# A two-block transformer step on one core: another order of DVE's work beside the keys and values, and side work ahead of the low half in 64 slots of a layer instead of 16

## The reference, cut to what matters

```python
for i in range(DEPTH):                                   # DEPTH = 2, "the layers"
    u = rms_norm(h, norm_g[i]); z = u @ w_in[i]
    o_a = mla_mixer(...)                                 # latent attention
    o_b = dsa_mixer(...)                                 # index scores, top 64 keys, attention
    o_c = diff_mixer(...)                                # difference of two attentions
    mixed = concat([o_a*silu(g_a), o_b*silu(g_b), o_c*silu(g_c)])
    h = h + mixed @ w_o[i]
    h = h + (p[i] @ w_ple[i]) * sigmoid(h @ w_pg[i])
h = rms_norm(h, final_g)
# second block
sh1, sc1, gt1, sh2, sc2, gt2 = split(silu(c) @ w_ada + b_ada)      # the "ada" rows, and
csh1, csc1, ...              = split(silu(c_ctx) @ w_ada + b_ada)  # the same for the context
rq, rk, rv, rg, mq, mk, mv, mo, mg, gr, gm = split_in(modulate(x, norm1_g, sh1, sc1) @ w_in)
crq, crk, ...                              = split_in(modulate(ctx, ...) @ w_in)
# retention scan and mLSTM scan, both directions; merge; then a PEER layer (top-16 experts)
```

## Time and profile before

| | us |
|---|---|
| three timed executions | 3944.96, 3946.69, 3958.2 |
| their median | 3946.69 |
| the profiled execution | 3957.74 |
| its span, first to last instruction | 3955.9 |
| PE busy in it | 3773.8 (95%) |
| DVE busy in it | 2352.2 (59%) |
| ACT busy in it | 1549.7 (39%) |

### The profile page before, as it was taken

The page is one execution under the profiler, slowest core; times in us unless marked ns, Lnnn a source line. Parts: engine busy times, 40 slices in busy tenths (PEclk is TensorE's granted clock), DMA queues, the critical chain, the costliest instruction groups (busy, mean ns, idle before and its releaser), DMA issues.

```text
span 3955.9 us, 49916 instructions
## 1 busy us (share of the span) xinstructions
PE 3773.8 (95%) x21042; PEld 3213.1 (81%) x21042; DVE 2352.2 (59%) x3127; ACT 1549.7 (39%) x1518; POOL 101.0 (3%) x145
## 2 busy tenths in 40 slices
PE   8999999999999679799999989999999999999998
PEld 6776777777777467697888889999999999988886
DVE  3455654436554366647664558867655565567777
ACT  3443544333443331125543343345533333333333
POOL 0000000000000000001000000000000000000000
PEclk8999999999999889899999999999999999999999
DMA  5545565645555436634356644555666666666664
GB/s 207 194 167 193 195 235 188 248 151 192 200 213 210 169 146 251 240 128 149 133 182 238 222 141 175 192 203 218 237 231 219 222 221 220 233 227 243 232 241 173
DMA packets 117959, 799.30 MB, mean 202 GB/s; under 512 B 13137, under 2 KB 13521, under 8 KB 29457
## 3 DMA queue, kind: packets, MB, share of 16 engines
q1 hardware_dynamic: 96704, 692.73, 48.3%
q0 software_dynamic: 18768, 82.96, 5.6%
q10 hardware_dynamic: 2304, 20.97, 1.3%
HBM read 752.57 MB, written 44.04 MB: 201 GB/s over the span
## 4 chain that ended last, share of the span: by engine, by line
PE 52%; DVE 6%; DMA 3%; ACT 2%; issue 2%; DVEq 0%; ACTq 0%; POOLq 0%; POOL 0%; SPq 0%
PE ps L289 16%; PE ps L291 16%; PE ps L290 16%; DMA ring<-in_stream_dram 3%; DVE ring_r L303 2%; PE ps L1676 1%; DVE z L2786 1%; ACT high L297 1%; PE ps L1535 1%; DVE z L3133 0%; DVE act L2897 0%; PE ps L1412 0%; PE ps L1484 0%; PE ps L1498 0%; DVE z L3129 0%
## 5 line engine op out<-in xcount | busy, mean ns | idle before, releaser
L297 ACT CAST high<-ring 128x2048 fp32r<-128x2048 f32 x384 | 733.7, 1912 | 1333.4 <-DMA ring<-in_stream_dram 1328.3
L303 DVE TENSOR_TENSOR ring_r<-ring,high 128x2048 fp32r<-128x2048 f32 x384 | 878.9, 2291 | 632.6 <-ACT high L297 629.0
L291 PE MATMUL ps<-high,act_r 128*128 128x512 f32 x1888 | 742.7, 393 | 0.0
L289 PE MATMUL ps<-high,z_r 128*128 128x512 f32 x1856 | 733.2, 395 | 1.4 <-DVE z L3251 1.2
L290 PE MATMUL ps<-ring_r,z_r 128*128 128x512 f32 x1856 | 727.3, 392 | 0.0
L290 PE MATMUL ps<-act_r,high 128*128 128x256 f32 x2496 | 707.8, 284 | 0.0
L2309 DVE TENSOR_TENSOR ring_r<-ring,high 128x2048 fp32r<-128x2048 f32 x176 | 402.6, 2290 | 458.4 <-ACT high L1784 456.8
L289 PE MATMUL ps<-act_r,high 128*128 128x256 f32 x2304 | 657.0, 285 | 9.8 <-DVE ring_r L303 9.4
L291 PE MATMUL ps<-act_r,ring_r 128*128 128x256 f32 x2304 | 652.9, 283 | 0.0
L289 PE MATMUL ps<-high,h_r 128*128 128x512 f32 x1472 | 598.7, 407 | 47.3 <-DVE ring_r L2309 17.6
L290 PE MATMUL ps<-ring_r,h_r 128*128 128x512 f32 x1472 | 579.4, 394 | 0.0
(11 more groups left out here) (474 smaller groups left out, 3172.3 us busy)
## 6 DMA issues: line engine op xcount, KB each, us to landing
ring<-in_stream_dram SPq DMA_DIRECT2D x656, 1024.0 KB, 4.8
hidden<-z POOLq DMA_DIRECT2D x32, 512.0 KB, 3.8
gate_matrix<-z ACTq DMA_DIRECT2D x8, 2048.0 KB, 6.4
r<-gate_matrix POOLq DMA_DIRECT2D x32, 512.0 KB, 6.7
z<-hidden POOLq DMA_DIRECT2D x32, 512.0 KB, 7.1
r<-in_w_ple_dram POOLq DMA_DIRECT2D x2, 2048.0 KB, 9.7
merge_gates<-r ACTq DMA_DIRECT2D x8, 512.0 KB, 5.1
r<-merge_gates POOLq DMA_DIRECT2D x4, 1024.0 KB, 5.2
```

What stands on the lines that cost most here:

```text
L289: pe.matmul(out, lhs[0], rhs[0], start=start, stop=False)
L291: return pe.matmul(out, lhs[1], rhs[0], start=False, stop=stop)
L297: sc.copy(high[:, j, :], ring[:, j, :]).then_inc(piece_high[j], 1)
L303: dve.tensor_tensor(ring_r[:, j, :], ring[:, j, :], high[:, j, :], ALU.subtract).then_inc(piece_low[j], 1)
```

## The change

There are four edits. First, in kv and mvmk DVE's work is written as one rule for every piece: after the low half of piece i+3 come a1(i+1) and a0(i+2), and then the low half of piece i+4. DVE's evacuation of a chunk stands behind the low half of the next chunk's first piece (before: of its second), and ACT's behind the cast of the next chunk's second piece (before: of its third). SP's loop is rewritten in the same form, and its list of transfers stays what it was. Second, `SIDE_FIRST` becomes 14 to 77. Third, the scan's first product no longer waits for `evac[1]`. Fourth, that wait stands before the transposes beside the scan's second piece.

```diff
-        SIDE_FIRST = range(38, 54)
+        SIDE_FIRST = range(14, 78)
...
+                        if q == 1:
+                            pe.wait_ge(evac[1], EVAC0["rgmo"])
                             turn_pairs(head_src, 8, 4, rt_full)
...
                         if c == 0:
                             pe.wait_ge(evac[0], e0)
-                            pe.wait_ge(evac[1], e0)
... ACT
-                    for m in range(4):
-                        split_act(sc, kv_chunk(m), (3,))
-                        split_act(sc, kv_chunk(m + 1), range(3))
-                        sc.wait_ge(piece_used[3], place(kv_chunk(m), 1, 1))
-                        out_kv(m // 2, m % 2)
+                    for i in range(PIECES - 1, kv_out_at(3)):
+                        split_act(sc, kv_chunk(i // PIECES), (i % PIECES,))
+                        m = (i + 1 - kv_out_at(0)) // PIECES
+                        if m >= 0 and i + 1 == kv_out_at(m):
+                            sc.wait_ge(piece_used[3], place(kv_chunk(m), 1, 1))
+                            out_kv(m // 2, m % 2)
... DVE
                     def stream_kv(m, evacuate):
-                        ada_part(m, 0, 0)
-                        low(m, 3)
-                        ada_part(m, 1, 0)
-                        ada_part(m, 0, 1)
-                        low(m + 1, 0)
-                        ada_part(m, 1, 1)
-                        ada_part(m, 0, 2)
-                        low(m + 1, 1)
-                        dve.wait_ge(piece_used[3], place(kv_chunk(m), 1, 1))
-                        evacuate()
-                        ada_part(m, 1, 2)
-                        ada_part(m, 0, 3)
-                        low(m + 1, 2)
-                        ada_part(m, 1, 3)
+                        for i in range(PIECES * m, PIECES * (m + 1)):
+                            ada_at(1, i + 1)
+                            ada_at(0, i + 2)
+                            low_at(i + PIECES)
+                            if i % PIECES == 0:
+                                dve.wait_ge(piece_used[3], place(kv_chunk(m), 1, 1))
+                                evacuate()
...
+                    ada_at(0, 0)
+                    low_at(PIECES - 1)
+                    ada_at(1, 0)
+                    ada_at(0, 1)
...
                     stream_kv(4, keep_early)
-                    split_dve(dve, kv_chunk(5), (3,))
                     split_dve(dve, kv_chunk(6), range(3))
```

More of the change, by code:

```diff
@@ L276, in ada_used, with kv_out_at @@
             return sum(kv_chunk(m)) + 2 + i
+        def kv_out_at(m):
+            return PIECES * (m + 1) + 2
         def ada_sums(n):
@@ L941, in load_ada, with load_at @@
                 sp.dma_start(ring[:, j, :], t["stream"][ada_place(ADA_L + 2 * m + i), j]).then_inc(piece_full[j], 16)
[L943 to L958, removed]
+            def load_at(i):
+                load_weights(i // PIECES, i % PIECES)
+            for i in range(PIECES - 1):
+                load_at(i)
+            load_ada(0, 0, 0)
+            load_at(PIECES - 1)
+            load_ada(0, 1, 0)
+            load_ada(0, 0, 1)
+            for i in range(KV_ADA * PIECES):
+                load_at(i + PIECES)
+                for n, at in ((1, i + 1), (0, i + 2)):
+                    if at < KV_ADA * PIECES:
+                        load_ada(at // PIECES, n, at % PIECES)
             with sp.Fori(2 * PAIR0["kv"] + ADA_CHUNKS + KV_ADA + 1, gates1) as c:
@@ L2057, in out_m @@
                                 sc.copy(raw_c[:, b, :], ps[:, b, 0:TOK]).then_inc(evac[1], 1)
[L2058 to L2062, removed]
+                    for i in range(kv_out_at(3), KV_ADA * PIECES + 2 * PIECES - 1):
+                        split_act(sc, kv_chunk(i // PIECES), (i % PIECES,))
+                        if i + 1 == kv_out_at(4):
+                            sc.wait_ge(piece_used[3], place(kv_chunk(4), 1, 1))
+                            out_m(0, 0)
+                    sc.wait_ge(piece_used[3], place(kv_chunk(5), 1, 1))
+                    out_m(0, 1)
                 elif name == "mqrq":
@@ L2789, in ada_part, with low_at, ada_at @@
                         a.then_inc(piece_used[j], 1)
-                    def stream_kv(m, evacuate):
-                        def low(c, j):
-                            split_dve(dve, kv_chunk(c), (j,))
-                        ada_part(m, 0, 0)
-                        low(m, 3)
-                        ada_part(m, 1, 0)
-                        ada_part(m, 0, 1)
-                        low(m + 1, 0)
-                        ada_part(m, 1, 1)
-                        ada_part(m, 0, 2)
-                        low(m + 1, 1)
-                        dve.wait_ge(piece_used[3], place(kv_chunk(m), 1, 1))
-                        evacuate()
-                        ada_part(m, 1, 2)
-                        ada_part(m, 0, 3)
-                        low(m + 1, 2)
-                        ada_part(m, 1, 3)
+                    def low_at(i):
+                        split_dve(dve, kv_chunk(i // PIECES), (i % PIECES,))
+                    def ada_at(n, i):
+                        if i < KV_ADA * PIECES:
+                            ada_part(i // PIECES, n, i % PIECES)
+                    def stream_kv(m, evacuate):
+                        for i in range(PIECES * m, PIECES * (m + 1)):
[5 more added lines that the diff above has]
+                                evacuate()
                     def out_kv(i, par):
```

## The result

The changed kernel takes 3915.15 us (median of 4 runs, 3911.2 to 3924.32) beside 3945.82 for the kernel before (4 runs, 3944.21 to 3958.2). The ratio is 0.9919 with the interval 0.9892 to 0.9946, a gain of 32 us by the ratio and 30.7 by the two medians. Forecast were 3908.7 and a ratio of 0.9904. The profiled execution took 3924.32 against 3957.74: 33.4 us less where 38.0 were forecast.

A forecast was written before the change was run, and what follows sets the result against it. PE, busy 95% of the span, bounds the kernel; gains come from its idle or half-clock stretches. 7.3 + 5.2 + 3.1 + 12.4 + 1.5 + 10.1 − 1.65 = 38.0 us, so 3946.69 − 38.0 = 3908.7, likeliest 3901 to 3917.

The forecast's parts named there:

- Part 1: Keys and values: ada parts ahead of the low half shorten a piece's round from 12.1 us; 7.3 us gained.
- the closed chain: Keys and values: a0, transfer of a1, a1 take 11.1 us a piece, just under PE's 11.24, so PE becomes the bound.
- Part 2: Sum after the 17th piece: wait for the last a1 goes, +5.2 us; sum begins at full clock, +3.1 us.
- The 3.7 us more: Sum of 64 one-column matmuls: if they count as busy, it stays at full clock and the forecast falls by 3.7 us.
- Part 3: Before mvmk's second half: PE's 14.40 us wait for ScalarE's copy falls to 2.0, gaining 12.4 us.
- The 1.5 for the restart: mvmk's second half: PE's half-clock restart after the 14.40 us wait also goes, +1.5 us (0 to 1.5).
- Part 4: Layers, side work first in slots 14 to 37 and 54 to 77: 3.9 − 5.3 + 8.2 + 3.3 = +10.1 us.
- Part 5: Scan's first product: its wait moves to the fourth piece, some 7 us there; gain 0, half-clock restart costs 1.65 us.
- A: Rival, keys and values: the ring still sets the round at 12.1 us; gain 24.7, time 3922; chance 0.14.
- B: Rival, layers: late low halves stall PE up to 2.65 us a slot, deciding from 14 more slots; slower; chance 0.04.
- C: Rival, better: the sum holds full clock (+3.7) and slot 33 costs nothing (+5.3); time 3899.7; chance 0.14.
- D: Rival: transfer order unchanged, so only part of Part 4 and the earlier copies count; 20.9 us, time 3925.8; chance 0.07.

The follow-up runs named there:

- e6: Changed kernel with one more DVE instruction (0.76 us) in every ada part, against the changed kernel; 3933.80 us, ratio 0.9967 to the kernel before.
- e7: Changed kernel with the sum's 64 one-column matmuls in four groups of 16 behind consecutive columns of products; 3913.62 us, ratio 0.9902 to the kernel before.
- e11: Kernel before with the chunks' evacuations one piece earlier on DVE and ACT, ada parts in old order; 3954.09 us, ratio 1.0015 to the kernel before.
- e5: Changed kernel with a chunk's evacuations back in their old places, one piece later, ada order new; 3926.45 us, ratio 0.9944 to the kernel before.
- e2: Changed kernel with side work first in slots 38 to 53 only, as before; 3915.34 us, ratio 0.9910 to the kernel before.
- e12: Changed kernel with only slots 18 and 37 turned beside 38 to 53; 3899.93 us, ratio 0.9873 to the kernel before.

## Why the prediction was right, and where it was off

The result lies in the range, and the likeliest case held. Point by point:

- **Part 1, the round.** Forecast 7.3; the waits fell from 8.2 to 0.7, four pieces take 45.20. e6 bears out the closed chain on which it rests, to 0.2 us a piece.
- **Part 2, the sum.** The wait of 5.2 us went. The sum fell from 13.79 to 10.70 us, 3.1 as taken. The 3.1 was a choice between bounds without a row for it, so that it fits is luck; in the nine profiles with this block it took 9.34 to 10.70 us. The clock begins at full and falls inside it (0.65 on the mean); it stays full when the block is spread (e7). The 3.7 us more did not come. The Trainium skill (TensorE: Matmul & The Clock Gate, Part 1: The HAM clock gate) lets the gate follow how busy the engine is; PE was busy in all of the block, and the clock fell all the same.
- **Part 3, the 14.40 us.** 12.4 forecast, 12.45 measured. The reason given, copies placed earlier, was half of it. Alone they leave 12.51 us of the wait (e11), and the new ada order alone leaves 13.15 (e5); only both together take it away. The 1.5 for the restart came in some executions (mvmk's second half started at 1.00 in e2, and its first 3.7 us had 0.66 in the changed kernel's profile, after the same 1.95 of idle time). Parts 1 to 3 together: 29.5 forecast, 29.35 measured.
- **Part 4, the layers.** Forecast 10.1; the trace has 7.3, and the mean of the traces 4.7. This is the step that failed in size. Slots 18 and 37 gave what was forecast (e12: 15 us, forecast 3.9 + 8.2 + 3.3 = 15.4). Slot 33 cost 1.35 and 2.57, 3.9 where 5.3 was forecast; in three of the eight traces it costs nothing in the first layer. Wrong was "In the other turned slots that I followed, the side work's inputs lay ready before the cast. I set them at 0": slot 61 costs 2.0 and 1.6, by the same mechanism as slot 33, and 34 costs once 33 is freed. Slot 32 waits 1.4 us longer in the first layer, but for a late piece. The sum also counted the restarts that go (3.3) but not those that come: a new stall brings one too, as behind the 2.57 us of slot 33 (clock 0.50 in the window below). The −10 kept as bound was near the 12 to 14 that e12 shows.

```profile
951.60:954.40 2.80, 2.80 (x7) 2.22 (x8) 2.73 (x10) 2.27 (x3) 0.00 (x0) 0.50 1.02 430
```

- **Part 5, the scan.** The wait moved to the fourth piece (6.71; "some 7") and cost the half-clock restart: −1.65 forecast, −1.6 in the ledger, −2.7 over all traces.
- **The rivals.** A is excluded by the 45.20: the 11.1 stays under PE's piece, and e6 shows what it costs when it doesn't. Of B, the mechanism is there in slots 33 and 61, and in 34 once 33 is freed, far from the 14 places at which it decides. C did not come: slot 33 costs, and the sum loses its clock. D is excluded by e5: DVE's order alone gives 18 us, with the same order in the queue of transfers. That the total came within 5 us of the forecast hides that part 4 fell short.

## What to carry to other kernels

Follow each turned or moved instruction to what it waits for, one by one: of 48 slots two gave everything, and others, 33 and 61 first, took a good part of it back. A wait that is moved earlier is free only if nothing that stands behind it on its engine feeds the ring; the same copies cost 5.6 us or gave 11.4, by whether the work queued behind them had been done. Count the restart behind each stall too: in e11 it was the whole loss. And where a later event is fixed by another engine, an idle stretch does less harm early, so that the slow restart of the clock lies inside the waiting time; here that was worth 2.7 us, by traces alone.

## What the runs showed of the hardware that was not expected

The stretch in which PE ran at half clock at the program's start differs from execution to execution, though PE was busy in it throughout. Windows of the changed kernel's profile and of e5's, whose instructions are the same there:

```profile
23.50:50.00 26.50, 26.50 (x83) 22.44 (x83) 9.17 (x9) 10.56 (x19) 1.64 (x2) 0.50 0.43 166
```

```profile
23.50:50.00 26.50, 26.50 (x145) 23.06 (x146) 9.61 (x10) 12.76 (x21) 1.64 (x2) 0.94 0.52 206
```

PE got through 83 instructions in one and 145 in the other, and the third wait for a low half ends at 106.5 or at 95.8 us. That is 10.7 us of difference with no part in any change, a third of the effect that was measured here, and close to the range of the changed kernel's runs (3911.2 to 3924.32). How much of that range it makes is not shown: the profiled execution of e5, with the short stretch, was the slowest of its five. The second thing is that a long row of one-column matmuls, back to back and without idle time, lost the full clock by itself, while groups of 16 among 512-column products kept it (e7). The changed kernel's windows inside the sum:

```profile
1610.10:1612.00 1.90, 1.90 (x19) 1.90 (x18) 0.15 (x1) 0.32 (x1) 0.00 (x0) 1.00 0.86 276
1612.00:1614.00 2.00, 2.00 (x17) 2.00 (x17) 1.89 (x4) 0.00 (x0) 0.00 (x0) 0.83 0.96 393
1614.00:1616.00 2.00, 2.00 (x11) 2.00 (x11) 0.95 (x2) 0.00 (x0) 0.00 (x0) 0.50 0.49 123
```

It fell from 2.4 to 1.2 GHz inside the block, after products at full clock and with no gap ahead of it.
